# The second block in two passes of 256 tokens, with plain fp32 projections, the second pass between the gathered rows of the first

## The reference, cut to what matters

```python
xn = rms_norm(x, ln_mix_g); proj = xn @ w_in              # 1024 -> 2560: u, v, q, k, v
a_out = gelu(u) * (w_s . rms_norm(gelu(v)) + b_s)         # w_s mixes tokens within blocks of 128
b_out = softmax(norm(q) . norm(k) / 8 + bias) . v         # 8 heads, causal by chunks of 64
x = x + concat(a_out, b_out) @ w_out
xf = rms_norm(x, ln_ffn_g); q = xf @ w_query              # 1024 -> 8 heads x 2 x 128
for each token and head: top 16 of 128 + top 16 of 128 scores, top 16 of the 256 sums,
    softmax g of these, eidx their expert numbers
h = gelu(expert_u[eidx] . xf)                             # 16384 experts, 1024 wide
x = x + sum over the 128 chosen of (g * h) * expert_v[eidx]
```

## Time and profile before

| | |
|---|---|
| median of 3 runs | 3746.68 us (3739.82 to 3754.43) |
| profiled execution | 3746.21 us, its span 3744.4 |
| mean granted TensorE clock | 0.925 |
| busy: PE / DVE / ACT / POOL | 84% / 46% / 22% / 20% of the span |
| HBM read | 1026.41 MB |
| start of the second block | near 2004 us |
| first gather issued, first dot | 2389.3, 2402.9 us |
| last row's matmuls end | near 3738 us |

### The profile page before, as it was taken

One profiled execution on the slowest core, in us unless ns is written; L12 is line 12 of the kernel. 1 busy time (PEld: TensorE's weight loads), 2 busy tenths in 40 slices (PEclk: granted clock), 3 DMA queues, 4 the chain that ended last, 5 costly groups with the idle time before them and its releaser, 6 DMA issues.

```text
span 3744.4 us, 34079 instructions
## 1 busy us (share of the span) xinstructions
PE 3155.2 (84%) x12422; PEld 1697.2 (45%) x12422; DVE 1726.0 (46%) x3643; ACT 837.3 (22%) x1867; POOL 747.8 (20%) x618
## 2 busy tenths in 40 slices
PE   7689979978779999999996978899878778877877
PEld 6478757725633333333334846433333333333332
DVE  3643574455510110011003463556767767767774
ACT  2223323332100000000003332222322222222221
POOL 0412322100000000000000000134444444444442
PEclk9889989869889999999998977999999998999999
DMA  2211220032399999999994200698999999999997
GB/s 105 75 62 35 70 70 1 31 127 110 126 380 419 419 420 420 420 420 420 420 420 195 78 23 12 237 377 333 408 420 420 420 420 414 420 420 407 420 420 320
DMA packets 150056, 1042.02 MB, mean 278 GB/s; under 512 B 16640, under 2 KB 18432, under 8 KB 27008
## 3 DMA queue, kind: packets, MB, share of 16 engines
q0 software_dynamic: 75408, 543.20, 35.3%
q1 hardware_dynamic: 74480, 496.65, 32.7%
HBM read 1026.41 MB, written 13.37 MB: 278 GB/s over the span
## 4 chain that ended last, share of the span: by engine, by line
PE 63%; DMA 15%; DVE 14%; ACT 4%; issue 2%; POOL 2%; DVEq 0%; SPq 0%; ACTq 0%; POOLq 0%
PE ps L91 60%; DMA gb<-in_peer_uv,eidx 13%; DVE gb L145 3%; PE ps L96 2%; POOL gb L85 2%; DVE inv_tt L114 1%; DMA ring<-in_wt 1%; DMA ga<-in_eu 1%; ACT diag L167 1%; DVE wa_hi L129 1%; DVE sq L133 1%; DVE wa_lo L114 1%; DVE expert_act L114 1%; DVE rw_t L133 1%; DVE prob L145 0%
## 5 line engine op out<-in xcount | busy, mean ns | idle before, releaser
L91 PE MATMUL ps<-gb,diag 128*128 128x512 f32 x2048 | 990.8, 637 | 266.8 <-ACT diag L167 265.0
L85 POOL DMA_INDIRECT gb<-in_peer_uv,eidx x512 | 565.9, 1105 | 1128.9 <-PE ps L91 680.9
L91 PEld LDWEIGHTS ps<-gb,diag 128*128 128x128 f32 x2048 | 400.4, 202 | 838.0 <-issue 432.7
L145 DVE CUSTOM_DVE_ANT_0 gb<-gb,xn 128x1024 f32<-128x1024 f32 x512 | 618.2, 1219 | 176.6 <-DMA gb<-in_peer_uv,eidx 174.8
L91 PE MATMUL ps<-ga,xt 128*64 128x512 f32 x1120 | 330.8, 600 | 2.5 <-DVE xt L119 2.5
L114 DVE TENSOR_TENSOR expert_act<-expert_act,ps 128x512 f32<-128x512 f32 x32 | 22.0, 687 | 541.9 <-PE ps L91 541.4
L114 DVE TENSOR_TENSOR x<-x,ps 128x512 f32<-128x512 f32 (+1 forms) x104 | 62.6, 605 | 382.6 <-PE ps L91 381.1
L167 ACT ACTIVATE dots<-dots 128x2 f32<-128x2 f32 (+1 forms) x304 | 61.8, 203 | 721.2 <-DVE dots L145 719.5
L167 ACT ACTIVATE diag<-cons,soft 128x128 f32<-128x128 f32 x512 | 205.6, 402 | 50.2 <-DVE onehot L114 0.4
L91 PEld LDWEIGHTS ps<-ga,xt 128*64 128x64 f32 x1120 | 118.6, 137 | 187.1 <-issue 179.2
L91 PE MATMUL ps<-h_hi,wa_hi 128*128 128x512 f32 x368 | 160.5, 436 | 39.5 <-DVE wa_lo L114 35.8
(11 more groups left out here) (325 smaller groups left out, 4435.9 us busy)
## 6 DMA issues: line engine op xcount, KB each, us to landing
ga<-in_eg SPq DMA_DIRECT2D x70, 1024.0 KB, 26.2
ga<-in_eu SPq DMA_DIRECT2D x70, 1024.0 KB, 27.1
ga<-in_ed SPq DMA_DIRECT2D x68, 1024.0 KB, 27.6
ring<-in_wt SPq DMA_DIRECT2D x55, 1024.0 KB, 5.2
gr<-in_eu SPq DMA_DIRECT2D x37, 1024.0 KB, 27.0
gr<-in_ed SPq DMA_DIRECT2D x34, 1024.0 KB, 27.7
ring<-in_eg SPq DMA_DIRECT2D x29, 1024.0 KB, 26.5
gr<-in_eg SPq DMA_DIRECT2D x29, 1024.0 KB, 27.1
```

The source lines that it names most:

```text
L85: self.e.indirect_dma_start(out, None, table, bass.IndirectOffsetOnAxis(ap=idx, axis=0)).then_inc(s, 16)
L91: i = self.e.matmul(out, l, r, start=st, stop=sp, skip_group_check=True)
L145: self.done(self.e.tensor_tensor_reduce(out=o, in0=a, in1=b, scale=scale, scalar=start, op0=o0, op1=o1, accum_out=acc), name)
```

## The change

It has these parts:

1. Mixer and attention become `sp_pass`, `pe_pass`, `ac_pass`, `dv_pass` for 256 tokens (p = 0 or 1), written as generators of some 50 steps. Pass 0 runs through. Pass 1 is advanced one step by each new event "m" of `peer_order`, two for every five rows from row 4 to 131. The query for its tokens follows as eight events "p", at rows 132 to 167.
2. The projections are plain fp32 matmuls of 256 columns; the halves and their conversions are gone. q and k come out by tokens; their head norms are done by tokens on DVE, and the result is transposed. The weight tiles are read once for each pass, from an array `wt2` of their own, in another order (q, k, v first, the gates last).
3. The gate's tiles are a filler in the attention loop, one tile for every second unit up to unit 6. The bias is read by head.
4. The buffers of gathered rows: 5 before `GROW` = 180, then 13.
5. A row's matmuls: the diagonal is taken as two blocks of 64x64. Rows 0 to 63 and 64 to 127 of the array each multiply their own tokens, 4 matmuls of 64x64 by 512 columns. For an odd row the outputs cross to the other 64 partitions, in two other banks; at the end of a block of tokens ACT copies the crossed sums (`crossed`) and PE adds them back (`total`).

```diff
-            return n % 8, (n - 8 if n >= 8 else None)
+            return n % 5, (n - 5 if n >= 5 else None)
@@ peer_order
-                if done % 13 == 0 and p < 16:
-                    yield ("p", p)
+                if done % 13 == 0 and p < 8:
+                    yield ("p", 0, p)
...
+            if 4 <= n < 132 and n % 5 in (1, 3):
+                yield ("m",)
+            if 132 <= n < 172 and n % 5 == 2:
+                yield ("p", 1, (n - 132) // 5)
@@ pe_peer
+            if ev[0] == "m":
+                next(second, None)
+            elif ev[0] == "p":
+                p, m = ev[1:]
+                s = TILES * p + P0 + m
                 b, use, before = turn.next()
+                w = w8(ring2(s))
+                pe.wait_ge(("tile2", s), ("f", p, 5), ("f", p, 7), *before)
+                for a in range(2):
+                    for k in range(8):
+                        pe.mm(PS[b][:, 256 * a:256 * a + 256], w[:, k, 128 * a:128 * a + 128], fT[:, k, :], k == 0, k == 7,
+                              ("used", s) if a and k == 7 else None)
...
                     for half in range(2):
-                        pe.mm(PS[VB[2 * (i % 2) + half]], diag[n % 4], rows_[:, 1024 + 512 * half:1536 + 512 * half], k == 0, k == 127,
-                              ("sum", n) if half else None)
+                        for r in range(2):
+                            to = r if k % 2 == 0 else 1 - r
+                            pe.mm(PS[VB[2 * (k % 2) + half]][64 * to:64 * to + 64, :], diag[n % 4][64 * r:64 * r + 64, 64 * r:64 * r + 64],
+                                  rows_[64 * r:64 * r + 64, 1024 + 512 * half:1536 + 512 * half], k < 2, k == 127,
+                                  ("sum", n) if half and r else None)
```

The attention loop of the new pass, on PE and DVE (unit u is head u // 2, token block u % 2 of the pass):

```diff
+        for u in range(19):
+            if u < 16:
+                h, j = UNITS[u]
...
+                n = 128 * (2 * p + j + 1)
+                pe.wait_ge(("q2", p, 1), ("k2", p, 1), *before)
+                pe.mm(PS[b][:, 0:n], q2[r, h // 2, 128 * j:128 * j + 128], k2_[r, h // 2, 0:n], name=("s_ps2", p, u))
+            if u % 2 == 0:
+                next(filler, None)
+                next(filler, None)
...
+            if 2 <= u < 18:
+                w = u - 2
...
+                pe.wait_ge(("prob", p, w), *before)
...
+            yield
@@ dv_pass
+                dv.ttr(Pb2[u % 3][:, 0:n], PS[b][:, 0:n], ab[h % 2][:, 384 - 128 * i:512], -1.0, 3.0e38, ADD, ALU.min, sm2(u)[0], name=use)
...
+            if 1 <= u <= 16:
+                w = u - 1
...
+                dv.wait_ge(("ae", p, w))
+                dv.recip(l, l)
+                dv.ts(P, P, l, MUL, name=("prob", p, w))
```

More of the change, by code:

```diff
@@ L1 @@
+import itertools
 import math
@@ L1713, in norm, with sm2, dv_pass, root @@
+    def sm2(u):
+        return small[:, 32 + u % 4:33 + u % 4], small[:, 36 + u % 4:37 + u % 4]
+    def dv_pass(dv, p, turn):
+        a, b_ = 2 * p, 2 * p + 1
+        def root(name, i, at):
+            q = st8[:, at:at + 1]
             dv.wait_ge((name, "sq", i))
@@ new lines, in mixed, with features @@
+        def mixed(i):
+            q = root("n3", i, 4 + i)
+            dv.ts(XN[:, i, :], X[:, i, :], q, MUL, name=("n3", i))
+        gain(a)
+        yield
+        gain(b_)
+        mixed(a)
+        yield
+        mixed(b_)
+        yield
+        def features(name, src, dst, kcol):
+            for c2 in range(4):
+                b, use, _ = turn.next()
+                if c2 % 2:
+                    dv.wait_ge((src, p, c2))
+                    for c in (2 * c2, 2 * c2 + 1):
+                        dv.ts(dst[:, c, :], PS[b][:, 256 * (c % 2):256 * (c % 2) + 256], col(kcol + c), MUL, name=(name, p, c))
+                    dv.mark(use)
+                    yield
@@ new lines, in dv_pass, with fill @@
+        turn.next()
+        yield
+        head_scale(1)
+        yield
+        for j in range(2):
+            b, use, _ = turn.next()
+            dv.wait_ge(("qk_ps", p, 0, j))
+            dv.ts(q2[:, :, 128 * j:128 * j + 128], PS[b].rearrange("p (a b) -> p a b", a=4), col(K_QN), MUL, 0.125, MUL, name=use)
+            dv.mark(("q2", p, j))
+        yield
+        turn.next()
+        yield
+        yield
+        turn.next(), turn.next()
+        yield
+        sc = st8[:, 8:10]
+        def fill():
+            for m in range(6, 10):
+                turn.next()
+                yield
+                yield
@@ new lines, in dv_pass @@
+        for m in range(O0, P0):
+            n = m - O0
+            b, use, _ = turn.next()
+            yield
+            dv.wait_ge(("used", TILES * p + m))
+            x = X[:, a:b_ + 1, 256 * n:256 * n + 256]
+            dv.tt(x, x, pair(PS[b]), ADD, name=use)
+            if n == 3:
+                dv.mark(("x_2", p))
+            yield
+        for i in (a, b_):
+            q = root("x3", i, i)
+            dv.ts(XN[:, i, :], X[:, i, :], q, MUL, name=("xn3", i))
+            yield
+        yield from features("f", "f_ps", fT, K_FFN2)
@@ L2018, in ac_peer @@
                         ac.wait_ge(("sum", n - 4))
-                    ac.act(diag[n % 4], ident, ACT.Copy, scale=soft[:, n // 128, n % 128:n % 128 + 1], name=("diag", n))
+                    ac.act(diag[n % 4], ident, ACT.Copy, scale=soft[:, n // 128 % 2, n % 128:n % 128 + 1], name=("diag", n))
+            elif ev[0] == "out":
+                i = ev[1]
+                ac.wait_ge(("sum", 128 * i + 127), ("dot", 128 * i + 127))
+                for half in range(2):
+                    ac.act(XN[:, i, 512 * half:512 * half + 512], PS[VB[2 + half]], ACT.Copy, name=("crossed", i))
     def dv_choose(dv, i, h):
```

726 lines of the change are left out of this document (413 added, 313 removed).

## The result

| | before | after | ratio, 95% interval |
|---|---|---|---|
| median of the runs, us | 3746.08 | 3875.73 (3873.16 to 3888.95) | 1.0352 (1.0320 to 1.0383) |
| profiled execution, span, us | 3744.4 | 3887.0 | |
| first dot | 2402.9 | 2229.9 | |
| dot of row 180 | 2891.5 | 3033.5 | |

The change makes the kernel 3.5% slower: 3875.7 us, above the range 3670 to 3870 and 90 above the 3786 forecast.

What follows compares the result with a forecast made beforehand. It took the first 80 rows as bound by TensorE and its chain, the last 332 by DMA. 3746.2 - 183 (row 0 earlier) + 220 (rows 0 to 179) + 3 (tail) = 3786 us; range 3670 to 3870.

Steps and rivals of the forecast that it cites:

- Term 1: Stretch before the first dot: the first pass alone, 256 tokens, takes 215 us against 398.5, so row 0 starts 183 earlier.
- Term 3: The last 332 rows, paced by DMA: unchanged at 2.5 us each, with 3 us more in the tail.
- Term 2: Rows 0 to 179, with the second pass interleaved: 709 us against 488.65 before, +220.
- At the 4 us a row below it does not bind: Rows 0 to 179: five gather buffers allow 2.7 us a row, so they set no limit.
- Rows and choice: 180 x 1.75: Rows 0 to 179: 1.75 us of matmul a row plus 11 head scores at 3.3, 351 us in all.
- 16 x 5.5: Second pass's attention: 16 steps of 5.5 us each, from a step's start to the next row's matmul.
- The steps hide: Rows 0 to 179: chains lie under TensorE's work, 561 us there, +72; 3638 to 3727 us in total; chance 0.28.
- The clock falls: Interleaved stretch: TensorE's clock at 0.71 lengthens 345 us of matmul by up to 117; 3830 to 3900 us; chance 0.19.
- Quarters in one bank do not overlap: All row matmuls: two diagonal quarters writing one PSUM bank take turns, 3.44 us a row; 4404 us; chance 0.05.
- First dot near 2220: Start of the gathered rows: a first dot near 2220 us would show the earlier start of row 0.
- Dot of row 180 near 2932: End of rows 0 to 179: this dot near 2932 us, 2891.5 before, would confirm the time forecast for them.
- Idle by diagonal over 100 us: Rows 4 to 131: TensorE idle over 100 us for ScalarE's diagonal would show the stalls; below 50, hidden steps.

Runs made afterwards that it cites:

- grow: The changed kernel with gather buffers added as the second pass frees memory (6 from row 74, 9 from row 127) instead of five to row 179: 3819.9 us.
- before5: The kernel before, with only five gather buffers and rows taken singly to row 179: 3874.2 us.
- upfront: The changed kernel with the first pass's eight query chunks and the whole second pass done before the first gathered row: 3908.1 us.
- upfront_grow: The changed kernel with eight query chunks and the whole second pass before the first row, and nine gather buffers from row 8: 3784.4 us.
- warm: The changed kernel with two extra matmuls that add zeros ahead of each row's wait for its diagonal, rows 4 to 127: 3887.3 us.
- notables: The changed kernel with the second pass's exponentials made gelus and its square roots copies, so they load no tables: 3865.7 us.
- nolag: The changed kernel with each row's weight, diagonal and matmuls right behind its own dot, not the next row's, in rows 0 to 179: 3896.3 us.
- before_quarters: The kernel before, with only the gathered rows' sums changed to 64 x 64 quarters of the diagonal: 3750.9 us, 0.9991.
- whole: The changed kernel with row matmuls as before, on the whole 128x128 diagonal, and no crossed sums: 3887.3 us.

## Why the prediction was wrong

**Term 1 was right.** Row 0 starts 173 us earlier; 183 forecast, with 170 to 216 as bounds. One reading in it is wrong without changing the sum: the 46.4 us from the first query tile to the first dot hold nearly seven chunks (114 records, 16 each) and not three. **Term 3 was right**: 853.5 against 852.9 us for the last rows, tail and all.

**Term 2 failed by 94 us**, 803.6 against 709. The prediction's prices laid out by rows:

| rows | forecast | after | grow |
|---|---|---|---|
| 0 to 15 | 74 | 65.7 | 65.0 |
| 16 to 50 | 131 | 142.9 | 135.5 |
| 51 to 98, attention | 214 | 253.0 | 249.3 |
| 99 to 131 | 124 | 138.0 | 127.8 |
| 132 to 171, query chunks | 145 | 179.6 | 140.9 |
| 172 to 179 | 21 | 24.4 | 19.7 |
| sum | 709 | 803.6 | 738.2 |

*The first failed step* is the sentence on the buffers, "At the 4 us a row below it does not bind". It has two faults. The way back was sized at 4.3 us from four instructions, without the order in which they are written: the weight stands behind the next dot, and it took 8.9. And I compared means, 2.7 us a row against 4. The rows don't come every 4 us; they come in bursts of four at 1.4 us behind a chunk or step of 7, the burst empties the five buffers, and the refill begins only then. So the buffers' wait and the steps add. It cost 127 us in the kernel before (before5), 125 with no step between the rows (upfront against upfront_grow), and 65 of the 94 here (grow, which has nine buffers at best). With more buffers the same prices hold outside attention: 489 against 495. A part of the 65 is the clock: with fewer waits the row matmuls of grow ran 122 us at 1.2 GHz instead of 169.

*The second* is a term that was mis-sized, the row at 1.75 us in "Rows and choice: 180 x 1.75", in attention. The stretch took 39 us more than its 214. Of these 26 lie in its 48 rows: 109.7 us, 2.3 a row, against 84. Sixteen attention steps took 121.3 against 112 with the tiles and gate matmuls that ride in them, 9 more; the rest is 3 us of a turning step that stands elsewhere in the table, and 1 of scores. So "16 x 5.5" was a little low (in the example VectorE's gate scaling, 0.77 us twice, stands ahead of the next dot), and it is not where the time went. The 1.75 is a row at the full clock, and 70.6 of the 108.6 us of row matmuls there ran at half of it. At the full clock they would have been up to 35 us shorter. That is worked out from the records and not shown by a run: warm, the run that raised the clock, lengthened the rows as much. The table loads (5 us of the stretch, notables) and the buffers (4, grow) are not it.

**The rivals.** *The steps hide* fell: upfront, with the second pass ahead of the rows, has its first dot 203 us later than after, and after's rows 0 to 179 cost 185 us more than upfront's. Both figures hold two query chunks (some 14 us) that after does later. So 18 us of a pass of 189 were hidden by laying it between the rows, a tenth. With nine buffers nothing was: the first dot of upfront_grow is 204.5 us later than grow's and its rows are 245 shorter, a part of which is that it has its nine buffers from row 8. *The clock falls* gave a range, 3830 to 3900, in which the result lies, and that is in part luck: it had the clock at 0.71 in the stretch and took for it all matmuls between the rows as well, while it was 0.87 (0.84 in attention), the steps' matmuls ran at 2.4 GHz nearly all the time (10 us at 1.2 in rows 0 to 179), and the largest loss is that of the buffers. But its mechanism is there, in the rows. *Its sign*, a clock under 0.85, was met in attention alone. *Quarters in one bank do not overlap* fell: 32 records in 5.52 us, 1.38 a row in a burst, below the 1.75 that I took. The Trainium skill's sentence in "TensorEngine Tiling (Array Packing)", Restrictions and Gotchas, that different row tiles can't access one bank at the same time does not hold here, where they write different 64-partition halves of it. Its "PSUM — Partial Sum Buffer", on bank collisions, has two writers collide by bank and quadrant, and with that the trace agrees; the same section quotes the stricter sentence too.

What the part was worth is another matter: the faster quarters, the only part that could have made up for something, gave 7 us in rows 0 to 179 of after, within the scatter of single profiles, and none in the kernel before, where the diagonal was late instead.

**The signs I had named.** First dot near 2220: 2229.9. Dot of row 180 near 2932: 3033.5, which put the miss in term 2. Idle by diagonal over 100 us: 217. DMA at 1.0 from row 175: yes. What was missing is the one that would have told of the buffers, the dots' idle time before landing gathers, 107 us.

**What stays open.** What the low clock costs: no run raised it without lengthening the rows. And whether a change to the order of work within a step (the dot ahead of attention's minimum on VectorE, the diagonal ahead of the exponential on ScalarE) would let the second pass hide at all; it wasn't tried.

## What to carry to other kernels

Compare a loop of buffers with the longest gap and burst around it, not with the mean pace: five buffers with a 16 us way round (landing, a dot, a row of lag, a matmul) give 3.2 us a row alone, and every step between the rows adds to that once a burst has emptied them. Moving work into a stretch whose three engines already take turns hid little: 18 of 189 us of the second pass, while 102 choice steps, nearly all on VectorE, cost 2.5 us in the pass. An edit that removes a wait can make another of its size (nolag), so look for the new one, and test a part by itself in the kernel before as well (before5): it told most for one run. And split a stretch by what TensorE does in it before naming the term that failed: here the steps, whose long chains catch the eye, cost less than forecast, and the rows more. A run that fills waits with work on the engine it tests (warm) measures the filling too.

## What the runs showed of the hardware

- Matmuls of 64 rows by 64 columns in diagonal quarters overlap though both write one PSUM bank, in different halves of its partitions. The eight records of row 150 of after start in pairs 7 ns apart, at 2913.09, 2913.57, 2914.00 and 2914.43. The two records of one 64-column matmul start one behind the other where it runs alone (2096.71 and 2096.98, 256 columns), so a pair is the two quarters of one half.
- A row by itself gains nothing from it: 1.94 us, four times 0.43 and the end of the last. In a burst the quarters of successive rows, which cross to the other partitions, overlap too: 32 records of 512 columns in 5.52 us, 1.38 a row, against 16 records of 128 x 128 in 7.13, 1.78 a row.
- A row by itself at the two levels of the clock, 1.94 and 3.6 us (rows 150 and 151 of after, columns as above):

```profile
2913.09:2915.03 1.94, 1.94 (x10) 0.47 (x8) 0.15 (x1) 0.00 (x0) 1.33 (x3) 1.00 0.59 135
2919.70:2923.30 3.60, 3.60 (x8) 0.76 (x8) 2.12 (x6) 0.00 (x0) 0.00 (x0) 0.50 0.99 410
```

- With the quarters the granted clock in the DMA-bound stretch fell from 0.93 to 0.81, with TensorE busy 534 of 853.5 us, and the stretch took the same time. The quarters alone do it: 0.82 in before_quarters, 0.93 in whole.
- A gather of 128 x 8 KB took 5.9 us from issue to its dot with no other on its way (after, 2911.73), and 7.7 with two ahead of it (upfront, 2612.86).
- 46 table loads of 1.28 us, 59 us of ScalarE, were worth 10 us.
